# A new opening, score products in groups of two and split last stores in a two-layer decoder trunk

## The chip, the cores and the metric

The kernel runs on one core of a Trainium2 chip. The metric is the device time of one execution in microseconds. The core has a matrix engine (TensorE, PE in the profile), whose products go to eight banks of accumulators (PSUM), three engines for element work (VectorE or DVE, ScalarE or ACT, GpSimd or POOL), and a further one, SyncE or SP, which here only issues transfers. ScalarE can issue transfers too, in between its own work. The engines run side by side, each in its own order, and wait for one another by semaphores.

## What is computed

A trunk of two layers on 512 tokens of 1024 features, in float32. Each layer is

```python
h = rmsnorm(x, norm_mix[l]);   x = x + hybrid_mixer(h, w_in[l], ...)
h = rmsnorm(x, norm_xattn[l]); x = x + cross_attention(h, rmsnorm(mem, norm_mem[l]), ...)
h = rmsnorm(x, norm_mlp[l]);   x = x + sq_relu_mlp(h, mlp_w1[l], mlp_w2[l])
```

and a last `rmsnorm` closes it. The mixer multiplies `h` with the wide matrix `w_in` and cuts the product into columns for four branches: an mLSTM (`m_q`, `m_k`, `m_v`, `m_o` and two narrow gates), GLA (`g_q`, `g_k`, `g_v`, `g_r` and the narrow `g_a`), an S5 state-space model (`s_u`) and HGRN2 (`r_q`, `r_f`, `r_i`, `r_g`). HGRN2 and GLA are the same linear attention with a decay for every key feature, in chunks of 64 positions:

```python
decay = exp(where(causal, g[t] - g[s], -inf))           # per key feature
att   = einsum('bhtk,bhsk,bhtsk->bhts', q, k, decay)
o     = einsum('bhtk,bhkv->bhtv', q * exp(g), S) + einsum('bhts,bhsv->bhtv', att, v)
```

The branches' outputs are projected, weighted by sigmoid gates, summed and projected once more.

## The kernel before

**Dense products.** Each float32 operand is split into a high and a low half, and a product is three (high by high, low by high, high by low). Weights come in units of 128x512 through a ring of nine slots, `WR`. SyncE loads them (L596 and on), ScalarE copies the high half (`feed`, L1429), GpSimd subtracts it to get the low half in two pieces (L694, L695). TensorE takes the units block by block (`parts`, `gemm`, `token_values`); a unit in the usual form gives 12 products, each of 128x512. The order of blocks is written out by hand in TensorE's program: `r_i` with `g_v`, `r_f`, `r_q`, `g_qk`, `g_r`, `r_g`, `gate3_0`, `m_q`, `m_k`, `m_v`, `m_o`, and so on. All products go through the helper at L701, so a line tells little there; the operands' names tell the place. VectorE's helpers for element work stand at L1965 to L1974.

**Opening.** Four tiles of 128 tokens of `x` come in two halves each: tiles 0 and 2 on SyncE's queue (L538), 1 and 3 on ScalarE's. On SyncE's queue there follow the `norm_mix` row (L540, behind a wait for a VectorE memset), unit 0 in two halves (L624: columns of `r_i` and of `g_v`), the second halves of tiles 0 and 2 (L641), then further units. TensorE turns the `norm_mix` row (L964) and the tiles (L944, `x_columns`: tile by tile for the first four groups of features, later group by group). ScalarE scales each turned group into `Uhi` (L1595), VectorE makes its low half and a copy of it (L1974, L2157). `token_values` multiplies groups 0 and 1 for two token tiles and asks for both halves of weights and data before its first product. ScalarE also sums the squares of `x` (L1602); VectorE turns the scales into a diagonal (L1971), which TensorE multiplies, and `h` comes out of that in eight groups: ScalarE's high half (`norm_hi`, L1493, each group behind the `feed` of one more unit, 8 to 15) and VectorE's low half. `values_out` (L1501) empties the banks of `r_i` and `g_v`; `r_f` needs the first of them and `h`.

**Parameters.** After unit 8, SyncE issues `mem`, the level masks and all small parameter rows of layer 0 (`param_rows`, L545 to L580), at their head two loads of `s5_log_step` (L547) that spread 8 numbers over 64 partitions, four bytes a piece; those of layer 1 come three with each unit from 13 to 21. TensorE turns the rows of layer 0 (`params`, L949) ahead of `r_f`, and needs all 23 loads. After unit 12 come two narrow columns of `w_in` (L634), after unit 14 three kinds of loads for the S5 and GLA parameters (L665).

**Level scores.** HGRN2 (`hg`) and GLA (`gl`) form `att` in seven levels: `level_diff` (VectorE), `level_exp` (ScalarE, L1540), `level_mul` (VectorE, L1965 and L1974), `scores` (TensorE, 32 small products a level from 1 up) and `pick` (VectorE, L2081, L2091), which copies the level's part into `att` and frees its banks. The scores stand between parts of dense blocks, one level at a place. After the last level ScalarE copies the turned keys of GLA (`kt_copy`), behind the last tanh of the mLSTM's convolution.

**End.** ScalarE scales the last `out` tiles' first half (L1957) and stores it (L1958), VectorE and SyncE do the second half (L2801, L685), one transfer for each tile and half.

## Time and profile before

| what | value |
|---|---|
| median of 3 runs | 1950.54 us (1949.77, 1950.54, 2742.4) |
| the profiled execution's own time | 1949.91 us |
| its span, first to last instruction | 1948.1 us |
| TensorE's granted clock, mean | 0.999 |
| busy share PE, DVE, ACT, POOL | 99%, 64%, 49%, 58% |

The span is what the trace holds; the time also has what lies around it, 1.8 us. Times in the rows are counted from the span's start. A row of the timeline is a run of like instructions with its start, its length, and in brackets the idle time before it and what ended it. Dense products overlap: a row of 0.39 us starts 0.23 us after the one before. The third run, 2742.4 us, stands apart from the other two.

### The profile page before, as it was taken

What the parts mean: (1) busy time and instruction counts of PE and PEld (TensorE: products, weight loads), DVE (VectorE), ACT (ScalarE), POOL (GpSimd) and SP (SyncE); (2) the same over time, 40 slices, a digit from 0 to 9 for tenths busy, and PEclk for the clock granted to TensorE, in tenths of its full rate; (3) what the DMA queues carried; (4) which work ended last, traced back from release to release, by engine and by line L of the source; (5) the groups of instructions that cost most, each with busy time, mean ns of one, the idle gap of its engine ahead of it and who ended that gap; (6) DMA issues with size and microseconds to landing.
All of it is one profiled execution on the core that took longest, in us unless ns stands there. A gap on an engine that the chain in (4) does not pass through costs nothing.

```text
span 1948.1 us, 33275 instructions
## 1 busy us (share of the span) xinstructions
PE 1931.3 (99%) x12707; PEld 1641.5 (84%) x12707; DVE 1249.7 (64%) x1909; ACT 961.8 (49%) x1665; POOL 1127.9 (58%) x1356
## 2 busy tenths in 40 slices
PE   7999999999999999999999999999999999999998
PEld 6788788888888889999887887888898888999997
DVE  5888778856145766767358786787641556667661
ACT  6754645345445644444456647353554655344334
POOL 4565564956834555766565555467576355566653
PEclk9999999999999999999999999999999999999999
DMA  6423233333422333333342233333343233333332
GB/s 187 119 73 85 82 83 88 87 109 107 148 82 81 99 99 102 99 103 98 98 102 79 72 87 82 81 83 87 120 130 124 66 98 95 111 104 98 103 98 81
DMA packets 196091, 191.41 MB, mean 98 GB/s; under 512 B 23834, under 2 KB 186204, under 8 KB 195548
## 3 DMA queue, kind: packets, MB, share of 16 engines
q1 hardware_dynamic: 194780, 187.19, 32.7%
q8 instruction: 101, 1.65, 0.3%
q10 hardware_dynamic: 1152, 2.10, 0.3%
q14 instruction: 58, 0.48, 0.1%
HBM read 185.04 MB, written 3.15 MB: 97 GB/s over the span
## 4 chain that ended last, share of the span: by engine, by line
PE 95%; ACT 2%; DVE 2%; DMA 1%; issue 0%; SPq 0%; POOL 0%; DVEq 0%; ACTq 0%
PE gemm L701 73%; PE mix L701 20%; DMA w_raw<-in_w_in_dram 1%; DVE work L1974 0%; DVE work L1965 0%; PE mix L1283 0%; DMA work<-in_norm_mix_dram 0%; DVE sums_raw L1965 0%; PE mix L944 0%; PE mix L1178 0%; ACT w_hi L1429 0%; ACT work L1819 0%; DMA w_raw<-in_mlp_w_dram 0%; PE mix L877 0%; ACT work_split L1579 0%
## 5 line engine op out<-in xcount | busy, mean ns | idle before, releaser
L694 POOL TENSOR_TENSOR w_lo<-w_raw,w_hi 128x256 fp32r<-128x256 f32 x676 | 584.8, 865 | 793.0 <-ACT w_hi L1429 793.0
L695 POOL TENSOR_TENSOR w_lo<-w_raw,w_hi 128x256 fp32r<-128x256 f32 x676 | 595.8, 881 | 0.0
L701 PE MATMUL gemm<-h_hi,w_hi 128*128 128x512 f32 x1248 | 493.7, 396 | 0.5 <-DVE h_lo L1974 0.5
L701 PE MATMUL gemm<-h_lo,w_hi 128*128 128x512 f32 x1248 | 486.2, 390 | 0.0
L701 PE MATMUL gemm<-h_hi,w_lo 128*128 128x512 f32 x1248 | 486.1, 390 | 0.0
L701 PE MATMUL gemm<-work_split,w_hi 128*128 128x512 f32 (+1 forms) x1552 | 446.9, 373 | 0.3
L1429 ACT ACTIVATE w_hi<-w_raw 128x512 fp32r<-128x512 f32 x676 | 380.0, 622 | 62.8 <-DMA w_raw<-in_w_in_dram 24.6
L701 PEld LDWEIGHTS gemm<-work_split,w_hi 128*128 128x128 f32 x1552 | 281.6, 189 | 51.0 <-DVE work_split L1974 1.1
L701 PE MATMUL gemm<-work_split,w_lo 128*128 128x512 f32 (+1 forms) x776 | 288.5, 372 | 0.0
L701 PEld LDWEIGHTS gemm<-h_hi,w_hi 128*128 128x128 f32 x1248 | 234.3, 188 | 56.7 <-issue 6.6
L701 PEld LDWEIGHTS gemm<-h_hi,w_lo 128*128 128x128 f32 x1248 | 234.3, 188 | 49.5
L701 PEld LDWEIGHTS gemm<-h_lo,w_hi 128*128 128x128 f32 x1248 | 234.5, 188 | 47.3 <-issue 1.0
L701 PEld LDWEIGHTS gemm<-work_split,w_lo 128*128 128x128 f32 x776 | 146.2, 188 | 25.4
L1427 ACT ACTIVATE gate_rows<-sums_raw 128x768 fp32r<-128x768 f32 x48 | 40.7, 848 | 196.5 <-DVE sums_raw L1965 196.5
L1965 DVE TENSOR_TENSOR work<-work 128x512 f32<-128x512 f32 (+5 forms) x142 | 124.7, 878 | 14.3 <-ACT work L1638 6.5
L701 PE MATMUL mix<-work_split,w_hi 128*128 128x256 f32 (+1 forms) x544 | 121.1, 286 | 0.2 <-DVE sums_lo L1974 0.2
L1965 DVE TENSOR_TENSOR x_t<-x_t,gemm 128x512 f32<-128x512 f32 x88 | 60.5, 687 | 92.0 <-PE gemm L701 87.0
L1534 ACT ACTIVATE gate_t<-gemm 128x512 f32<-128x512 f32 x52 | 31.1, 599 | 140.5 <-PE gemm L701 140.1
L701 PE MATMUL mix<-work_split,gate_rows 128*128 128x256 f32 x456 | 97.8, 283 | 0.0
L701 PEld LDWEIGHTS mix<-work_split,w_hi 128*128 128x128 f32 x544 | 91.8, 191 | 3.6 <-issue 1.4
L701 PEld LDWEIGHTS mix<-work 64*64 64x64 f32 (+4 forms) x3136 | 76.9, 128 | 17.7 <-issue 14.4
L701 PE MATMUL mix<-work 64*64 64x64 f32 (+8 forms) x3136 | 84.2, 231 | 0.9 <-DVE work L1974 0.6
(372 smaller groups left out, 2792.9 us busy)
## 6 DMA issues: line engine op xcount, KB each, us to landing
w_raw<-in_mlp_w_dram SPq DMA_DIRECT2D x256, 256.0 KB, 2.7
w_raw<-in_w_in_dram SPq DMA_DIRECT2D x208, 256.0 KB, 2.7
w_raw<-in_xattn_w_kv_dram SPq DMA_DIRECT2D x64, 256.0 KB, 3.0
w_raw<-in_w_branch_dram SPq DMA_DIRECT2D x32, 256.0 KB, 2.7
w_raw<-in_w_out_dram SPq DMA_DIRECT2D x32, 256.0 KB, 2.7
w_raw<-in_xattn_w_q_dram SPq DMA_DIRECT2D x32, 256.0 KB, 2.8
w_raw<-in_xattn_w_o_dram SPq DMA_DIRECT2D x32, 256.0 KB, 2.7
w_raw<-in_w_in_dram SPq DMA_DIRECT2D x32, 128.0 KB, 3.5
```

Source lines behind the costliest of these rows:

```text
L694: pool.tensor_tensor(lo[:, 0:half], raw[:, 0:half], hi[:, 0:half].bitcast(F32), ALU.subtract)
L695: pool.tensor_tensor(lo[:, half:], raw[:, half:], hi[:, half:].bitcast(F32), ALU.subtract).then_inc(split_ready, 1)
L701: return pe.matmul(o, w, a, start=start, stop=stop, skip_group_check=True)
L1427: act.activation(SWhi[d // 2 % 2], SWraw[d // 2 % 2], ACT.Copy)
L1429: act.activation(hi, raw, ACT.Copy).then_inc(split_hi, 1)
L1534: do(act.activation(t[:, b, :], G[s][b][:, :], ACT.Tanh, scale=0.5), th_ready)
L1965: do(dve.tensor_tensor(o, a, b, op), s)
```

## The change

- *First copies.* The `norm_mix` row and the second half of unit 0 are issued by ScalarE, ahead of the second halves of tiles 1 and 3; SyncE no longer waits for the memset. The second halves of tiles 0 and 2 come behind unit 1. TensorE starts with 2.5 float32 products of zeros (`keep_busy`, on an operand that VectorE clears), turns tiles 0, 1, 3 and then 2, and ends with one more product of zeros. In layer 0 `opening` takes the products of groups 0 and 1 by kind (all high by high, then low by high, then high by low), each kind behind its own wait.
- *Transfers.* The four `s5_log_step` loads and the two narrow columns of layer 0 move to ScalarE, between the feeds up to unit 7 and those of units 8 and 9. The parameter rows are spread: five behind each of units 8 to 11, those of layer 1 two behind each of 15 to 24. `mem` comes behind unit 11, the masks behind unit 25 (VectorE waits for them before its first `pick`), the S5 and GLA loads behind unit 26. In layer 0 `norm_hi` feeds a unit behind each copy, not ahead of it, and four groups come before `values_out("r_i")`, not two.
- *Groups of two.* `scores` of levels 1 and 2, 3 and 4, 5 and 6 stand together, in both mixers, and VectorE's work is put in that order. `kt_copy(gl)` stands ahead of the last tanh.
- *End.* The last tile's scaling and stores are cut in two pieces of 256 columns on both paths.

```diff
+        def pieces(t):
+
+            return (slice(0, 512),) if t < TT - 1 else (FIRST, SECOND)
...
-            sp.wait_ge(p_vec, 1)
-            sp.dma_start(Rf(24, 1)[0:KC, 0:P], norm_mix[0].rearrange("(a b) -> a b", b=P)).then_inc(p_x[0], 16)
...
-                for a in range(2):
-
-                    src = s5_log_step[l].rearrange("(t a) -> a t", a=2)[a:a + 1, :]
-                    sp.dma_start(SM[64 * a:64 * a + 64, 16 + 8 * l:24 + 8 * l],
-                                 src.to_broadcast([64, 8]), allow_slow_non_contiguous=True).then_inc(landed, 16)
-                    yield
...
-                        for n in range(2):
+                        for n in range(2 if u else 1):
...
-                    if u == 12 or (L < DEPTH - 1 and (name, part) == ("up1_0", 0)):
-                        nl = L if u == 12 else L + 1
+                    if L < DEPTH - 1 and (name, part) == ("up1_0", 0):
+                        nl = L + 1
...
-                    if u == 0:
+                    if u == 1:
...
                     if u == 8:
+                        sp.wait_ge(p_pe, 1)
+                        rows0, rows1 = param_rows(0, p_rows), param_rows(1, p_x[1])
+                    if 8 <= u < 12:
+                        for _ in range(5):
+                            next(rows0, None)
+                    if u == 11:
                         sp.dma_start(R(20, 4).rearrange("p (t a) b -> p t (a b)", t=2),
                                      mem[0].rearrange("(t p) d -> p t d", p=P)).then_inc(p_rows, 16)
-                        sp.dma_start(LM[:, :, :], level_masks.rearrange("p (l c) -> p l c", c=CH)).then_inc(p_rows, 16)
-                        sp.wait_ge(p_pe, 1)
-                        for _ in param_rows(0, p_rows):
-                            pass
-                        rows1 = param_rows(1, p_x[1])
                         sp.wait_ge(p_pe, 7)
-                    if 13 <= u < 22:
-                        for _ in range(3):
+                    if 15 <= u < 25:
+                        for _ in range(2):
                             next(rows1, None)
+                    if u == 25:
+                        sp.dma_start(LM[:, :, :], level_masks.rearrange("p (l c) -> p l c", c=CH)).then_inc(p_dma, 16)
                     if u == UNIT["gate3_0"]:
                         sp.wait_ge(p_act, 3)
                         sp.dma_start(mem_scratch, YR[:, 0:4, :].rearrange("p a b -> p (a b)")).then_inc(p_out, 16)
-                    if unit == (14 if L == 0 else 10):
+                    if unit == (26 if L == 0 else 10):
...
-                sp.wait_ge(p_vec, PRO_VEC + TT + t + 1)
-                sp.dma_start(out[0, t * P:(t + 1) * P, 512:], R(2 * t + 1)[:, 0, :]).then_inc(p_out, 16)
-            sp.wait_ge(p_out, 16 + 2 * 16 * TT)
+                for n, at_ in enumerate(pieces(t)):
+                    sp.wait_ge(p_vec, PRO_VEC + TT + t + n + 1)
+                    sp.dma_start(out[0, t * P:(t + 1) * P, 512 + at_.start:512 + at_.stop], R(2 * t + 1)[:, 0, at_]).then_inc(p_out, 16)
+            sp.wait_ge(p_out, 16 + 2 * 16 * (TT + 1))
...
+                def opening(kc, tiles):
+
+                    u, banks = u0 + kc, [(G[(s0, s1)[t // 2]][t % 2][:, :], slice(t * P, t * P + P)) for t in tiles]
+                    w_hi, w_lo = WHi[:, u % RING, :], WLo[:, u % RING, :]
+                    pe.wait_ge(u_hi, kc + 1)
+                    pe.wait_ge(split_hi, u + 1)
+                    for o, tok in banks:
+                        mm(o, Uhi[:, kc, tok], w_hi, start=kc == 0, stop=False)
+                    pe.wait_ge(u_ready, kc + 1)
+                    for o, tok in banks:
+                        mm(o, Ulo[:, kc, tok], w_hi, start=False, stop=False)
+                    pe.wait_ge(split_ready, u + 1)
+                    for o, tok in banks:
+                        mm(o, Uhi[:, kc, tok], w_lo, start=False, stop=False)
...
-                products(0, (0, 1))
-                products(1, (0, 1))
+                for kc in range(2):
+                    if now[0]:
+                        products(kc, (0, 1))
+                    else:
+                        opening(kc, (0, 1))
...
-            pe.wait_ge(p_x[0], 48)
-            pe.transpose(G[0][0][:, 0:P], Rf(24, 1)[:, 0:P], ident).then_inc(p_pe, 1)
-            for t in range(TT):
-                if t:
-                    pe.wait_ge(p_x[t], 16)
-                if t < TT - 1:
-                    x_columns(t, range(4), XB)
-                else:
-                    for k in range(4):
-                        x_columns(t, (k,), XB).then_inc(p_pe, 1)
+            def keep_busy(n):
+                for _ in range(n):
+                    mm(G[1][1][:, :], MG[:, 7, 0:P], MG[:, 7, :])
+
+            pe.wait_ge(v_chain, 1)
+            keep_busy(2)
+            mm(G[1][1][:, 0:256], MG[:, 7, 0:P], MG[:, 7, 0:256])
+            for t in (0, 1, 3):
+                pe.wait_ge(p_x[t], (32, 16, 16, 32)[t])
+                if t == 3:
+                    pe.transpose(G[0][0][:, 0:P], Rf(24, 1)[:, 0:P], ident).then_inc(p_pe, 1)
+                x_columns(t, range(4), XB)
+            pe.wait_ge(p_x[2], 16)
+            for k in range(4):
+                x_columns(2, (k,), XB).then_inc(p_pe, 1)
+            keep_busy(1)
...
+                block = parts("r_g", *H)
+                some(block, 2)
                 pe.wait_ge(*of_layer(gl.gate_in, 2))
                 scores(hg, 1)
-                block = parts("r_g", *H)
-                some(block, 2)
                 scores(hg, 2)
                 rest(block)
-                scores(hg, 3)
                 block = gate_parts(3, 0)
                 some(block, 2)
+                scores(hg, 3)
                 scores(hg, 4)
                 rest(block)
-                scores(hg, 5)
                 block = parts("m_q", *H)
                 some(block, 2)
+                scores(hg, 5)
...
-                scores(gl, 1)
                 block = parts("m_o", *H)
                 some(block, 3)
+                scores(gl, 1)
                 scores(gl, 2)
                 rest(block)
                 branch_gemm(3, 0)
-                scores(gl, 3)
                 block = gate_parts(3, 1)
                 some(block, 3)
+                scores(gl, 3)
                 scores(gl, 4)
                 rest(block)
                 branch_gemm(3, 1)
                 block = gate_parts(3, 2)
-                some(block, 1)
+                rest(block)
                 scores(gl, 5)
-                rest(block)
                 scores(gl, 6)
...
             def norm_hi(k0, k1):
                 for k in range(k0, k1):
-                    feed(first_unit("r_i") + 8 + k)
+                    if now[0]:
+                        feed(first_unit("r_i") + 8 + k)
                     act.wait_ge(*of_layer(hx_ready, k + 1))
                     do(act.activation(Hhi[:, k, :], TH[:, k % 2, :] if now[0] else M[1 + k % 2], ACT.Copy), hi_ready)
+                    feed(first_unit("r_i") + 8 + k)
 
...
+            act.wait_ge(p_vec, 1)
+            act.dma_start(Rf(24, 1)[0:KC, 0:P], norm_mix[0].rearrange("(a b) -> a b", b=P)).then_inc(p_x[3], 16)
+            act.dma_start(WR[:, 0, BW:], w_in[0][0:P, COL["g_v"]:COL["g_v"] + BW]).then_inc(raw_in[0], 16)
...
+                if L == 0:
+                    feed(first_unit("r_i") + 8)
+                    for l, landed in ((0, p_rows), (1, p_x[1])):
+                        for a in range(2):
+                            src = s5_log_step[l].rearrange("(t a) -> a t", a=2)[a:a + 1, :]
+                            act.dma_start(SM[64 * a:64 * a + 64, 16 + 8 * l:24 + 8 * l],
+                                          src.to_broadcast([64, 8]), allow_slow_non_contiguous=True).then_inc(landed, 16)
+                    for what, wide, to in (("m_i", 8, 0), ("g_a", RANK, 8)):
+                        src = w_in[0][:, COL[what]:COL[what] + wide].rearrange("(k p) c -> p k c", p=P)
+                        act.dma_start(NW[:, :, to:to + wide], src, allow_slow_non_contiguous=True).then_inc(nw_in, 16)
+                    feed(first_unit("r_i") + 10)
+                first = 6 if L else 4
...
+                        kt_copy(gl)
                     act.wait_ge(*of_layer(ms["cv_ready"], j + 1))
                     do(act.activation(MTHG[j], MQK[j], ACT.Tanh, scale=0.5), ms["mth_ready"])
-                kt_copy(gl)
...
+                for at_ in pieces(t):
+                    do(act.activation(R(2 * t)[:, 0, at_], R(2 * t)[:, 0, at_], ACT.Copy, scale=SM[:, 32 + t:33 + t]))
+                    act.dma_start(out[0, t * P:(t + 1) * P, at_], R(2 * t)[:, 0, at_]).then_inc(p_out, 16)
...
+            do(dve.memset(MG[:, 7, :], 0.0))
...
+                if L == 0:
+                    dve.wait_ge(p_dma, 32)
...
-                pick(hg, 1)
                 level_diff(hg, 4)
                 gate_out("g_r", gl.GR)
                 level_mul(hg, 3)
+                level_mul(hg, 4)
+                pick(hg, 1)
                 pick(hg, 2)
                 level_diff(hg, 5)
-                level_mul(hg, 4)
-                pick(hg, 3)
                 level_diff(hg, 6)
                 gate_out("r_g", hg.GR)
                 level_mul(hg, 5)
+                level_mul(hg, 6)
+                pick(hg, 3)
                 pick(hg, 4)
-                level_mul(hg, 6)
                 last_decay(hg)
+                decayed(hg)
                 pick(hg, 5)
-                decayed(hg)
...
                 level_mul(gl, 1)
+                level_mul(gl, 2)
                 pick(gl, 0)
                 level_diff(gl, 3)
-                pick(gl, 1)
+                level_diff(gl, 4)
                 do(dve.tensor_copy(pr(17), Ur[:, S5_T, :]))
```

## Rows read from the trace of the kernel before

**Rows 1.** page, part 1: busy time, share of the span and instructions of each engine

```profile
PE 1931.3 (99%) x12707; PEld 1641.5 (84%) x12707; DVE 1249.7 (64%) x1909; ACT 961.8 (49%) x1665; POOL 1127.9 (58%) x1356
```

**Rows 2.** waits of PE, whole run: engine, line, what for; us in total, times, longest

```profile
PE gemm L964 <- DMA work<-in_norm_mix_dram: 7.5, 1, 7.5
...
PE mix L701 <- DVE work L1974: 0.6, 2, 0.3
...
PE mix L701 <- issue: 0.4, 2, 0.2
...
PE mix L701 <- DVE params_all L2211: 0.3, 1, 0.3
```

**Rows 3.** timeline of PE from 7 us: start, length, instructions, idle before and its end

```profile
7.73 3.28 PE L944 MATMUL mix<-consts_sb,work 128*128 128x128 f32 x16
...
12.31 0.50 PE L701 MATMUL gemm<-w_hi,work_split 128*128 128x512 f32 x1 [1.31 <-DVE merged_split L1974]
...
15.91 1.04 PE L944 MATMUL mix<-consts_sb,work 128*128 128x128 f32 x8
```

**Rows 4.** timeline of PE, 37 to 48 us

```profile
37.75 0.47 PE L701 MATMUL gemm<-h_hi,w_hi 128*128 128x512 f32 x1
...
47.42 0.50 PE L701 MATMUL gemm<-h_hi,w_hi 128*128 128x512 f32 x1 [0.54 <-DVE h_lo L1974]
```

**Rows 5.** transfers issued near 1.64 and from 2.6 us: KB each, median us to landing

```profile
work<-in_x_dram SPq DMA_DIRECT2D x1, 256.0 KB, 5.6
...
w_raw<-in_w_in_dram SPq DMA_DIRECT2D x2, 128.0 KB, 5.7
```

**Rows 6.** windows: stretch, length, busy PE PEld DVE ACT POOL, clock, DMA share, GB/s

```profile
7.46:10.50 3.04, 3.04 (x14) 3.04 (x15) 0.17 (x1) 0.63 (x1) 0.81 (x2) 1.00 1.08 386
```

**Rows 7.** timeline of ACT in the opening

```profile
10.72 1.41 ACT L1595 ACTIVATE work_split<-mix,params_all 128x512 fp32r<-128x512 f32 x2 [1.10 <-PE mix L944]
...
12.16 0.63 ACT L1429 ACTIVATE w_hi<-w_raw 128x512 fp32r<-128x512 f32 x1
...
30.62 0.60 ACT L1493 ACTIVATE h_hi<-mix 128x512 fp32r<-128x512 f32 x1 [4.83 <-DVE mix L1974]
```

**Rows 8.** timeline of POOL in the opening

```profile
9.69 0.73 POOL L694 TENSOR_TENSOR w_lo<-w_raw,w_hi 128x256 fp32r<-128x256 f32 x1 [9.25 <-ACT w_hi L1429]
```

**Rows 9.** timeline of DVE in the opening

```profile
24.02 2.74 DVE L1971 TENSOR_SCALAR work<-consts_sb,small 128x128 f32<-128x128 f32 x4
...
31.41 0.69 DVE L1974 SCALAR_TENSOR_TENSOR h_lo<-mix,h_hi 128x512 fp32r<-128x512 f32 x1
```

**Rows 10.** timeline of SP, 32 to 41 us

```profile
32.85 1.29 SPq L547 DMA_DIRECT2D small<-in_s_log_step_dram  x2
...
35.57 4.88 SPq L555 DMA_DIRECT2D work<-in_norm_mem_dram  x1
```

**Rows 11.** transfers in the window from 35 to 40 us: packets and bytes

```profile
DMA packets 542, 0.00 MB, mean 0 GB/s; under 512 B 542, under 2 KB 542, under 8 KB 542
```

**Rows 12.** timeline of PE around a group of HGRN2's scores

```profile
96.65 0.39 PE L701 MATMUL gemm<-h_hi,w_lo 128*128 128x512 f32 x1
...
96.97 1.15 PE L701 MATMUL mix<-work 128*64 128x64 f32 x32
...
98.05 0.50 PE L701 MATMUL gemm<-h_hi,w_hi 128*128 128x512 f32 x1
```

**Rows 13.** timeline of PE, GLA's scores of level 2

```profile
170.65 0.69 PE L701 MATMUL mix<-work 64*64 64x64 f32 x32
```

**Rows 14.** timelines of DVE and ACT, 157 to 168 us

```profile
157.43 1.91 DVE L2081 COPY_PREDICATED work<-masks_sb,mix 128x256 f32<-128x256 int32 x4
...
162.46 0.63 ACT L1540 ACTIVATE work<-work 128x512 f32<-128x512 f32 x1
...
165.58 1.72 DVE L1974 SCALAR_TENSOR_TENSOR work<-work,consts_sb 128x256 f32<-128x256 f32 x2
```

**Rows 15.** timeline of ACT at the end

```profile
1944.08 0.72 ACT L1957 ACTIVATE work<-work,small 128x512 f32<-128x512 f32 x1
```

More of the change, by code:

```diff
@@ L947, in params @@
             def params(l):
-                pe.wait_ge(p_x[1] if l else p_rows, 16 * 22 if l else 16 * 23)
+                pe.wait_ge(p_x[1] if l else p_rows, 16 * 22)
                 pe.transpose(M[3 - l][:, 0:P], Rf(24 + l, 1)[:, 0:P], ident).then_inc(p_pe, 1)
@@ L1599, in _ @@
                     t = k - 1
-                    act.wait_ge(p_x[t], 48 if t == 0 else 16)
+                    act.wait_ge(p_x[t], (32, 16, 16, 32)[t])
                     act.wait_ge(p_x2, 16 * TT)
@@ L1611, in _ @@
                 factors(0)
-                first = 6 if L else 2
+                if L == 0:
[10 more added lines that the diff above has]
+                first = 6 if L else 4
                 norm_hi(0, first)
@@ L1618, in _ @@
                 if L == 0:
-                    act.wait_ge(p_rows, 16 * 23)
+                    act.wait_ge(p_rows, 16 * 22)
                     for t in range(2):
@@ L1956, in _ @@
                 fdo(act.activation(SM[:, 32 + t:33 + t], SM[:, 32 + t:33 + t], ACT.Exp, scale=-0.5))
-                do(act.activation(R(2 * t)[:, 0, :], R(2 * t)[:, 0, :], ACT.Copy, scale=SM[:, 32 + t:33 + t]))
-                act.dma_start(out[0, t * P:(t + 1) * P, 0:512], R(2 * t)[:, 0, :]).then_inc(p_out, 16)
+                for at_ in pieces(t):
+                    do(act.activation(R(2 * t)[:, 0, at_], R(2 * t)[:, 0, at_], ACT.Copy, scale=SM[:, 32 + t:33 + t]))
+                    act.dma_start(out[0, t * P:(t + 1) * P, at_], R(2 * t)[:, 0, at_]).then_inc(p_out, 16)
         @block.vector
@@ L2300, in _ @@
                 tt(Ui[:, :, :], Ui[:, :, :], PS[:, 8:8 + S5_T + 1, :], ALU.mult)
-                level_mul(gl, 2)
-                level_diff(gl, 4)
-                pick(gl, 2)
                 tt(pr(5), re_, re_, ALU.mult)
@@ L2318, in _ @@
                 level_mul(gl, 4)
+                pick(gl, 1)
+                pick(gl, 2)
                 level_diff(gl, 5)
                 level_diff(gl, 6)
-                pick(gl, 3)
                 merge(3, 0)
@@ L2324, in _ @@
                 conv(1)
-                pick(gl, 4)
                 level_mul(gl, 5)
                 level_mul(gl, 6)
+                pick(gl, 3)
+                pick(gl, 4)
                 def silu_of(j):
@@ L2334, in _ @@
                 conv(2)
+                merge(3, 1)
                 pick(gl, 5)
                 decayed(gl)
-                merge(3, 1)
+                pick(gl, 6)
                 conv(3)
@@ L2340, in _ @@
                 silu_of(1)
-                pick(gl, 6)
                 decayed_queries(gl)
@@ L2800, in _ @@
                 dve.wait_ge(p_act, PRO_ACT + t + 1)
-                dve.scalar_tensor_tensor(out=R(2 * t + 1)[:, 0, :], in0=M[t], scalar=SM[:, 32 + t:33 + t], in1=GAINS[1],
-                                         op0=ALU.mult, op1=ALU.mult).then_inc(p_vec, 1)
+                for at_ in pieces(t):
+                    dve.scalar_tensor_tensor(out=R(2 * t + 1)[:, 0, at_], in0=M[t][:, at_], scalar=SM[:, 32 + t:33 + t], in1=GAINS[1][:, at_],
+                                             op0=ALU.mult, op1=ALU.mult).then_inc(p_vec, 1)
 _INS = ['x', 'mem', 'norm_mix', 'w_in', 'mlstm_conv_w', 'mlstm_conv_b', 'mlstm_i_bias', 'mlstm_f_bias', 'mlstm_norm',
```

## The prediction

> **What bounds the kernel now.** I read the page's first part, then who TensorE waited for over the whole run, then the order of time around each edited place. TensorE has work in flight for 1931.3 of 1948.1 us [rows 1], and the waits left to it are the reader's first surprise: 7.5 us for the `norm_mix` row before its first instruction, 0.3 us for `params_all`, 0.6 us in two waits for a VectorE product, 0.4 us in two waits before the turned keys' products [rows 2], and 0.5 us for the last low half of `h` [rows 4]. The rest is pace: products of 128x512 start about 0.23 us apart. So this kernel can only gain by starting its dense stretch sooner, by losing fewer steps where one kind of product follows another, and by a shorter end. All of that together is about 1% of the time; 2% of 1950 us is 39 us, more than the edited stretches hold.
>
> The opening has three places to see. The first 16 turns of `x` take 3.28 us, the next 8 only 1.04 us, so the first ones ran at half pace; the first dense product starts at 12.31 us, after a wait of 1.31 us for the low half, and its group of 12 ends at 15.91 us [rows 3]. The block `r_f` starts at 37.75 us and stands still once, 0.54 us before 47.42 us [rows 4]; between those TensorE keeps its pace.
>
> **The change, part by part.**
>
> *First copies.* The second half tile of `x` on SyncE's queue is issued at 1.64 us and lands 5.6 us later, at 7.2 us; the two halves of weight unit 0, issued behind the `norm_mix` row, land at the median 5.7 us after issues at 2.5 and 2.9 us, at 8.0 and 8.9 us [rows 5]. Afterwards the `norm_mix` row and the second half are on ScalarE's queue, ahead of the rest of `x`, and SyncE waits for nothing. How soon unit 0 is then complete no row shows: 7.2 us is the lower bound (with the tile ahead of it), 8.9 us the upper. I take 7.8 us, 256 KB at the 386 GB/s that the stretch from 7.46 us moves [rows 6] behind the tile. ScalarE copies unit 0 (0.63 us) and the first turned tile (0.7 us, half of the two in 1.41 us [rows 7]) and is done at 9.2 us instead of 11.4. `opening` starts with the products that need no low halves, but its last pair needs unit 1's low half: ScalarE copies tile 1 and unit 1 until 10.5 us and GpSimd takes two halves of 0.73 us after it [rows 8], so the group of 12 ends near 12.6 us, not 15.91: **3.3 us sooner**. The early zero products cost nothing: by the columns of the first turns (3.28 us for 16 x 128 [rows 3]) their 1280 columns take 2.1 us, or 4.1 if each column costs double, and with VectorE's memset of their operand early in the run both fit ahead of 7.2 us; what they may give is the better pace of the last four turns, 0.4 us, which is in this sum. Should they not lift the pace, the sum loses these 0.4 us. If unit 0 comes at 8.9 us, the gain is 2.2 us.
>
> *The rest of the opening.* TensorE would come to `r_f` at 37.75 - 3.3 = 34.4 us. On the way it needs the diagonal that VectorE builds until 26.76 us [rows 9] out of ScalarE's squares, which move up by some 1.7 us. TensorE gains 3.3, so the diagonal's slack of today shrinks by 1.6 us. TensorE does not wait for it today [rows 2]; I count nothing, and up to 1.6 us if there is no slack.
>
> *Six more issues on ScalarE.* ScalarE now idles 4.83 us before the first `h` copy at 30.62 us [rows 7]. Into that hole go unit 7, four `s5_log_step` loads, two narrow columns of `w_in`, and units 8 and 9. Its copies up to there are one string behind the first turned tile, so it comes to the first issue 1.3 to 2.2 us sooner than it came to the hole at 30.62 - 4.83 = 25.8 us: at 24.5 us, to take the later. Every issue holds the engine, and behind it stand the four `h` copies, then `values_out("r_i")`, which frees the bank that `r_f` writes: TensorE waits for that. The lower bound of the six: six at the pair's 0.64 us, 3.9 us [rows 10], so units 8 and 9 (1.25 us) end at 29.6 us, before the first `h` copy begins today: nothing is lost. But what TensorE also awaits for `params(0)`, the landing of the first two loads, is slow: in five microseconds only 542 packets move, 108 per us, while two such loads have 1024 [rows 11], so they need 9.5 us and land at 24.5 + 1.5 (the estimated way in) + 9.5 = 35.5 us; `r_f` starts then, 2.3 us sooner than now. The upper bound: an issue behind such loads can stick. SyncE's fourth issue after the pair (the sixth of six) took 4.88 us and ended at 40.45 us, 7.6 us after the first of the pair began [rows 10]. ScalarE has four of these loads and two larger lists behind them. If it is held until the third or the fourth load is through (1536 or 2048 packets at 108 per us), it is free at 40.2 or 45 us. The row nearest to this case is the 4.88 us one, because there too the sixth issue of a string follows these loads: I take a hold until 24.5 + 7.6 = 32.1 us. Units 8 and 9 then last to 33.4, the first `h` copy to 34.0, VectorE's pairs of passes (0.69 us each [rows 9], 1.45 a pair with their gaps) put the fourth copy at 37.5, and the first bank is free at 38.3 us: `r_f` **0.55 us later** than now.
>
> *After `r_f` has started.* The wait of 0.54 us inside it [rows 4] goes, about 0.7 us with the drain and refill around it: `h` no longer waits for unit 14, since ScalarE copies the units behind `h` and not ahead of it, and the slow loads have left SyncE's queue. The 0.3 us for `params_all` goes too, since ScalarE has done the squares of `mem` before `r_f` ends. The loads moved behind units 25 and 26 (masks, `s5_b`, `s5_c`, `WA2`) are issued as the units ahead of them get their slots, well before the block `g_r` whose masks and scores need them: nothing, unless that queue is late by a whole block. That opening in all: 0.55 - 0.7 - 0.3 = **-0.45 us**.
>
> *Groups of two.* A group of 32 score products today costs more than its own work: the product ahead takes 0.32 instead of 0.23 us, the first behind 0.50 instead of 0.39, and the group 1.08 us from 96.97 to 98.05, of which some 0.15 is the wait for its last product to end [rows 12]. GLA's groups are shorter, 0.69 us [rows 13], with the same two borders. A second group appended to a first spares one such border: 0.20 us for the two steps, 0.32 with a last product's end. Each layer has three places fewer for each of the two mixers: 12 x 0.32 = **3.8 us** (bounds 2.4 and 3.8). The odd level now comes later, so that its operands are never late: the two waits of 0.3 us for a product (0.35 each with the drain) go. `pick(gl, 6)` and ScalarE's copy of the turned keys stand ahead of a conv and a tanh, so the two waits of 0.2 us go. Together **1.1 us**. What could replace them: both levels 1 and 2 of GLA must be ready where level 2 stands today, 170.65 us, less the 0.8 us by which level 1 no longer stands ahead [rows 13]. ScalarE's exponent for level 2 ends at 163.1 us; VectorE's product for it (2.6 us: three passes, of which two take 1.72) and the pick of 1.91 us end at 167.6 us [rows 14]: some 2 us to spare.
>
> *Last stores.* The scaling of the last tile takes 0.72 us from 1944.08 us [rows 15]. In halves of some 0.4 us the first store goes 0.3 us sooner and the last about 0.5 us later with a quarter of the 512 KB behind it instead of all, which take 1.36 us at the 386 GB/s of [rows 6]. Between a loss of 0.5 and a gain of 0.7 I take **0.4 us** gained, because the second piece is issued while the first is moving.
>
> The sum: -0.45 - 3.8 - 1.1 - 0.4 = -5.75 us against the profiled execution's 1949.91 us, which lies between two of the runs shown (1949.77 and the median 1950.54; the third, 2742.4, is no measure of the program): **1944.2 us**.
>
> **The rivals.** *ScalarE is hardly held* (A). For it: its own queue has been empty since the last of `x`, and the pair's two issues took 1.29 us together [rows 10]. Then `r_f` starts at 35.5 us: -2.3 - 1.0 - 5.3 = -8.6, 1941.3 us.
> *ScalarE is held long* (C), which ends on the other side: free at 40.2 or 45 us, `r_f` at 46.4 or 51.2, 8.7 or 13.5 us later, less 6.3 for the rest: +2.4 or +7.2, 1952 or 1957 us. It decides from the point where the six issues last 14 us, ScalarE free at 38.2 and `r_f` at 44. For it speaks that there are twice as many slow packets as in the row; against it that SyncE was let go when half of them were through.
> *The order of transfers moves nothing* (D). For it: the DMA engines are already full at 386 GB/s when unit 0 lands [rows 6], so more queues bring no more bytes. Then the first dense group stays at 12.31 us, ScalarE has its issues in today's hole, and what is left is the waits of 0.7 and 0.3 and the 5.3 us: 1943.6 us, if that hole still holds them. Against it: it is not the bytes but the place of the `norm_mix` row and of the second half that changes. The Trainium skill has a rule for it, "DMA: Bandwidth & Descriptors", section "Issuing engines are not separate DMA queues": loads from several engines share the same DMA engines, and spreading them saves only issue time. By that rule the time would be this rival's. The row of the pair speaks half against it: what was queued behind it on the same queue waited, which the rule alone does not tell.
> *A pair waits* (E): the product for levels 1 and 2 of GLA comes 2 us past its slack in both layers: +4, 1948 us.
>
> **How the numbers follow.** The forecast 0.35, A 0.32, C 0.16 (half of it under 1951 us), D 0.07, E 0.05, something not seen 0.05. The forecast's own range is 1942.5 to 1947. For 8 in 10 the range goes down to 1939.5 (A with unit 0 at its lower bound) and up to 1951 (most of C's shorter holds left in). All cases stay within 2%, what a measurement of this kernel can tell from no change: faster 0.01, same 0.97, slower 0.02, these two for what is not seen.
>
> **What would show it.** Right: `r_f` starting at 38 us with ScalarE's issue rows stretched to some 7 us in all; 128x64 groups of 64; no wait of TensorE for a product near 177 us. A is right if those rows end by 28.5 us. The forecast is wrong if TensorE's first dense group ends after 14 us, if ScalarE's rows end after 38 us, or if a new wait stands at a pair.

## The result

The changed kernel takes 1956.62 us (median of 6 runs, 1954.94 to 1957.65), the kernel before 1950.01 us (median of the 6 runs now at hand; one of them, 2742.4 us, stands apart). The ratio is 1.0034 with a 95% interval of 1.002 to 1.0048: the kernel became slower by 0.34%, some 6.6 us. Forecast were 1944.2 us, and the range ended at 1951. Within 2% of the kernel before it stays, as said. The profiled execution took 1957.61 us with a span of 1955.8 us, 7.7 us more than before.

Where TensorE now waits, over the whole run (columns: engine, line, what for; us in total, times, longest), where [rows 2] has before:

```profile
PE gemm L702 <- ACTq L1529: 12.4, 1, 12.4
PE mix L968 <- DMA small<-in_s_log_step_dram: 3.0, 1, 3.0
PE gemm L702 <- DVE merged L2185: 1.8, 1, 1.8
PE mix L702 <- DVE sums_lo L2015: 0.3, 1, 0.3
```

All the small waits of [rows 2] are gone, and one new place costs 15.4 us. L968 turns the parameters, L1529 is ScalarE's signal at the end of `values_out("r_i")`. Both stand ahead of `r_f`. The timeline of PE there, against the first of [rows 4]:

```profile
37.71 0.45 PE L968 MATMUL mix<-consts_sb,work 128*128 128x128 f32 x1 [3.00 <-DMA small<-in_s_log_step_dram]
50.57 0.79 PE L702 MATMUL gemm<-h_hi,w_hi 128*128 128x512 f32 x1 [12.41 <-ACTq L1529]
51.16 0.63 PE L702 MATMUL gemm<-h_lo,w_hi 128*128 128x512 f32 x1
...
54.57 0.44 PE L702 MATMUL gemm<-h_hi,w_hi 128*128 128x512 f32 x1
54.85 0.40 PE L702 MATMUL gemm<-h_lo,w_hi 128*128 128x512 f32 x1
```

`r_f` starts at 50.57 us, not 37.75 [rows 4], and its first nine products start 0.43 us apart, not 0.23. The windows of the same stretch (stretch, length, busy PE PEld DVE ACT POOL, clock, DMA share, GB/s) show why the latter:

```profile
37.70:50.57 12.87, 0.45 (x2) 0.17 (x2) 4.82 (x7) 4.63 (x8) 3.37 (x5) 0.50 0.37 85
50.57:54.57 4.00, 4.00 (x9) 3.13 (x10) 3.33 (x6) 3.68 (x7) 2.65 (x5) 0.50 0.00 0
54.57:60.00 5.43, 5.43 (x25) 4.47 (x24) 3.47 (x6) 5.18 (x10) 3.81 (x6) 0.99 0.31 71
```

While TensorE stood still its granted clock went to 0.50, and it stayed there for the first 4 us of work: 1.85 us more than before over those products.

What held ScalarE, in its timeline (against [rows 7]):

```profile
23.68 2.86 ACTq L1646 DMA_DIRECT2D small<-in_s_log_step_dram  x4
26.58 17.17 ACTq L1650 DMA_DIRECT2D work<-in_w_in_dram  x2
43.80 1.15 ACT L1453 ACTIVATE w_hi<-w_raw 128x512 fp32r<-128x512 f32 x2 [19.50 <-issue]
44.85 1.21 ACT L1518 ACTIVATE h_hi<-mix 128x512 fp32r<-128x512 f32 x2
```

The four step loads were issued in 2.86 us, the two narrow columns in 17.17 us. Only then came units 8 and 9 and the first `h` copy, at 44.85 us instead of 30.62. What moved meanwhile, in the window from 28 to 34 us (packets of all queues; then queue, packets, MB, share of 16 engines; then a transfer with its size and us to landing):

```profile
DMA packets 680, 0.03 MB, mean 6 GB/s; under 512 B 658, under 2 KB 677, under 8 KB 680
...
q10 hardware_dynamic: 656, 0.00, 4.8%
...
w_raw<-in_w_in_dram SPq DMA_DIRECT2D x2, 256.0 KB, 16.7
```

ScalarE's queue (q10) moved 656 packets of four bytes in 6 us, 109 per us, the pace of [rows 11]; they fill 4.8% of the 16 DMA engines' time. (A packet in this view is a piece of a transfer in the text.) The two weight units that SyncE issued in that stretch (14 and 15) landed 16.7 us after their issue, at the median.

Since the dense products come in the same order but for the first twelve, their starts can be subtracted one from another. After minus before, in us:

| at | after - before | step |
|---|---|---|
| end of the first dense group (12.76 against 15.91) | -3.15 | the opening |
| first product of `r_f` | +12.81 | ScalarE held, TensorE stopped: +16.1 from -3.28 |
| tenth product of `r_f` | +14.66 | half clock: +1.85 |
| behind the place of the 0.54 us stop | +14.05 | stop gone: -0.6 |
| ahead of `g_r`'s second part | +13.56 | `params_all` and small steps: -0.5 |
| behind layer 0's groups | +10.72 | -2.84 |
| ahead of layer 1's groups | +10.57 | -0.15 |
| behind layer 1's groups | +7.72 | -2.85 |
| end of the span | +7.7 | some 0.2 lost on the way, the stores -0.2 |

So all parts but one gain about what was worked out, 10 us together, and one loses 18.

### The profile page after: what moved, and what is told of

Read it like the earlier page. It is cut to its first block, busy times and chain, and to the rows that moved or that the text cites. A ratio compares the mean times of both kernels' runs of the same rounds, so it can differ in the third digit from the quotient of the medians.

```text
span 1955.8 us, 33296 instructions
## 1 busy us (share of the span) xinstructions
PE 1932.7 (99%) x12715; PEld 1643.4 (84%) x12715; DVE 1248.0 (64%) x1911; ACT 959.9 (49%) x1666; POOL 1118.5 (57%) x1356
## 3 DMA queue, kind: packets, MB, share of 16 engines
HBM read 185.04 MB, written 3.15 MB: 96 GB/s over the span
## 4 chain that ended last, share of the span: by engine, by line
PE 96%; ACTq 1%; DVE 1%; ACT 1%; DMA 0%; issue 0%; DVEq 0%
PE gemm L702 74%; PE mix L702 20%; ACTq L1650 1%; PE mix L1307 0%; DVE sums_raw L2006 0%; ACT w_hi L1453 0%; PE mix L1202 0%; DVE work L2015 0%; DMA w_raw<-in_mlp_w_dram 0%; ACT work L1859 0%; PE mix L896 0%; ACT work_split L1605 0%; ACTq L1646 0%; DVE h_raw L2006 0%; PE mix L1396 0%
## 5 line engine op out<-in xcount | busy, mean ns | idle before, releaser
L695 POOL TENSOR_TENSOR w_lo<-w_raw,w_hi 128x256 fp32r<-128x256 f32 x676 | 580.6, 859 | 810.5 <-ACT w_hi L1453 810.5
L696 POOL TENSOR_TENSOR w_lo<-w_raw,w_hi 128x256 fp32r<-128x256 f32 x676 | 588.0, 870 | 0.0
L1453 ACT ACTIVATE w_hi<-w_raw 128x512 fp32r<-128x512 f32 x676 | 379.3, 621 | 75.6 <-issue 19.5
L702 PEld LDWEIGHTS gemm<-work_split,w_lo 128*128 128x128 f32 x776 | 146.2, 188 | 25.5
```

Source lines behind the costliest of these rows:

```text
L695: pool.tensor_tensor(lo[:, 0:half], raw[:, 0:half], hi[:, 0:half].bitcast(F32), ALU.subtract)
L696: pool.tensor_tensor(lo[:, half:], raw[:, half:], hi[:, half:].bitcast(F32), ALU.subtract).then_inc(split_ready, 1)
L702: return pe.matmul(o, w, a, start=start, stop=stop, skip_group_check=True)
L1453: act.activation(hi, raw, ACT.Copy).then_inc(split_hi, 1)
```

## The experiments

All ratios are to runs of the kernel before on the same chip (medians 1949.99, 1950.31 and 1950.21 us for the three groups of four).

**Who issues, and what stands ahead.** Three kernels put issues of the changed kernel back to SyncE; the fourth keeps all six on ScalarE and changes the shape of the step loads.

*e1: all six back on SyncE, at the places they had before.*

```diff
 def param_rows(l, landed):
+    for a in range(2):
+        sp.dma_start(SM[64*a:64*a+64, ...], <every second number of s5_log_step[l], spread over 64>)
...
-    if L < DEPTH - 1 and (name, part) == ("up1_0", 0):
+    if u == 12 or (L < DEPTH - 1 and (name, part) == ("up1_0", 0)):   # narrow columns
...
-    act.dma_start(...)   # six issues of ScalarE
```

> The changed kernel with the four step loads (4-byte pieces) and the two narrow columns issued by SyncE again, at the places they had before; all else as changed. In the changed trace ScalarE's two narrow issues last 17.2 us and r_f starts at 50.57 us, 16.1 us behind the 34.5 at which TensorE was ready, and 1.85 us more go at half clock after the stop. Theory H (what costs is that ScalarE is held in its issues): both go, 1956.6 - 16.1 - 1.85 = 1938.7 us, or 1942 if r_f still waits for the first step loads until 37.7. Rival S (the 4-byte pieces make every transfer late, whichever engine issues them): the weight units 9 and 10, now on the same queue, are late as before, r_f starts after 45 us, 1951 us or more.

Measured: 1941.81 us, ratio 0.9958 (0.9941 to 0.9974). TensorE's waits of the run, but for its start:

```profile
PE mix L707 <- DVE params_all L2250: 1.0, 1, 1.0
PE mix L707 <- DVE work L2003: 0.4, 1, 0.4
```

`r_f` starts at 35.06 us without a stop, and the time is far under the 1951 of S. It lies between H's two values, near the upper, but not for that value's reason: no wait for the step loads came. Of the 3.1 us over the lower value the two waits shown are 1.4; the rest is not traced.

*e2: the step loads on SyncE, the narrow columns on ScalarE.*

> The changed kernel with only the four step loads back on SyncE; ScalarE still issues the two narrow columns between units 7 and 8. Theory H, with the cause that the narrow lists wait behind 4-byte pieces on their own queue: their two issues take some 1.1 to 4 us, r_f starts between 34.5 and 38 us, 1939 to 1942 us. Rival N (a list of 1024 short pieces holds its issuer by itself): the two issues last about 17 us as now, r_f near 50, 1955 us.

Measured: 1941.42 us, ratio 0.9956 (0.9941 to 0.9971). ScalarE's timeline:

```profile
23.81 1.58 ACTq L1650 DMA_DIRECT2D work<-in_w_in_dram  x2
```

The same two issues that lasted 17.17 us last 1.58 us. Rival N falls: a narrow list alone holds nobody.

*e3: the narrow columns on SyncE, the step loads on ScalarE.*

> The changed kernel with only the two narrow columns back on SyncE, behind unit 12; ScalarE issues the four step loads. Theory H: ScalarE's issues take 2.9 us as now and it is free at 26.6 us; r_f waits for the first two step loads alone, near 37.7 us, 1942 us. Rival S: unit 9, which ScalarE copies ahead of h, lands at 41.9 us as now because the 4-byte pieces delay it on the other queue; r_f then starts at about 41.9 + 6.8 = 48.7 us, 1954 us. Rival N gives what H gives.

Measured: 1947.56 us, ratio 0.9987 (0.9978 to 0.9996), between the two theories. ScalarE's issues, and TensorE's timeline at `r_f`:

```profile
23.83 4.01 ACTq L1646 DMA_DIRECT2D small<-in_s_log_step_dram  x4
```

```profile
38.39 0.45 PE L968 MATMUL mix<-consts_sb,work 128*128 128x128 f32 x1 [3.51 <-DMA small<-in_s_log_step_dram]
38.59 0.77 PE L702 MATMUL gemm<-h_hi,w_hi 128*128 128x512 f32 x1
```

ScalarE is free at 27.84 us, 1.2 us later than H says: its fourth step load took 1.89 us, against 0.70 in the changed kernel. The course is H's: `r_f` waits for the first two step loads alone, 3.5 us, and then runs at half clock for some products, 2.4 us by the products' starts. H left out that second price and 0.8 us of a wait for `params_all`; from e4 below, which has none of the three, 1939.95 + 3.5 + 2.4 + 0.8 = 1946.7 us, 0.9 us under the measured median (two more small waits, 0.2 and 0.3 us, are in this trace and not in e4's). S was worked out with a wrong reading, in e1 as here: the units that land late are not 9 and 10 but 13 and 14, which ScalarE copies behind `h` and `r_q` needs. What S says of them is so: unit 13, issued from 25.82 us on, landed at 48.26 us. It was only not needed sooner.

*e4: the step loads in whole rows, all six on ScalarE as changed.* VectorE picks every second number while it copies.

```diff
-src = s5_log_step[l].rearrange("(t a) -> a t", a=2)[a:a + 1, :]
-act.dma_start(SM[64 * a:64 * a + 64, 16 + 8 * l:24 + 8 * l], src.to_broadcast([64, 8]), ...)
+act.dma_start(SM[64 * a:64 * a + 64, 16 * l:16 * l + 16],
+              s5_log_step[l].rearrange("(a b) -> a b", a=1).to_broadcast([64, 16]))
...
-dve.tensor_copy(PTA[:, l, step:step + 8], SM[:, 16 + 8 * l:24 + 8 * l])
+for a in range(2):
+    dve.tensor_copy(PTA[64 * a:64 * a + 64, l, step:step + 8], <columns a, a + 2, ... of SM[64 * a:64 * a + 64, 16 * l:16 * l + 16]>)
```

> The changed kernel with each step load made of whole rows: 64 pieces of 64 bytes in place of 512 of 4, issued at the same place by ScalarE, and VectorE picks every second number when it copies them. If the 4-byte pieces are the cause (H with them, and S): ScalarE's six issues take about 4 us, nothing is late, r_f starts at 34.5 to 36 us, 1939 to 1941 us. Rival N: the narrow lists hold ScalarE as now, 1955 us.

Measured: 1939.95 us, ratio 0.9949 (0.9934 to 0.9963): the fastest, 10 us under the kernel before and 16.7 under the changed one. ScalarE's issues, TensorE's two waits of the whole run, and `r_f`:

```profile
23.98 2.58 ACTq L1645 DMA_DIRECT2D small<-in_s_log_step_dram  x4
26.59 1.70 ACTq L1649 DMA_DIRECT2D work<-in_w_in_dram  x2
```

```profile
PE gemm L702 <- DVE merged L2184: 1.8, 1, 1.8
PE gemm L702 <- ACT work_split L1624: 0.5, 1, 0.5
```

```profile
34.86 0.27 PE L968 MATMUL mix<-consts_sb,work 128*128 128x128 f32 x1
35.24 0.50 PE L702 MATMUL gemm<-h_hi,w_hi 128*128 128x512 f32 x1
```

Same engine, same place, same order, as many issues: only the pieces of the step loads differ, 64 a load in place of 512, and VectorE's short copies of them. The stop and the half clock are gone. The cause is the 4-byte pieces. It is not their number alone, since in e2 two lists of 1024 pieces of 32 and 64 bytes held nobody; whether it is their size or that they take every second number of the source no run separates.

**How long a queue of them holds its issuer.** The two narrow issues of the changed kernel, one by one:

```profile
26.58 7.80 ACTq L1650 DMA_DIRECT2D work<-in_w_in_dram  x1
34.42 9.33 ACTq L1650 DMA_DIRECT2D work<-in_w_in_dram  x1
```

Counted in the trace, they ended when some 2120 and 2170 pieces were open, that is, issued and not yet moved (the packets that report a landing have four bytes too and are counted with them). Two kernels try the count.

*e9: the two narrow columns ahead of the four step loads.*

> The changed kernel with the two narrow columns issued ahead of the four step loads, all on ScalarE at the same place. Counted in the changed trace, 954 and 1924 of the 4-byte pieces had moved when the first and the second narrow issue ended, at 34.38 and 43.75 us: 3072 - 954 = 2118 and 4096 - 1924 = 2172 pieces were then issued and not yet moved. Theory R (an issuer is let go when no more than about 2150 pieces of its queue are open): the narrow pieces, which moved at some 500 a microsecond, make room, ScalarE is free by 32 us, and r_f waits for the landing of the first two step loads, 39 to 41 us, plus some 2 us of half clock: 1944 to 1947 us. Rival L (an issue waits for all that stands ahead of it in the queue to land): the last step load waits for three others, 14 us, ScalarE free at 40 us or later, r_f at 47, 1953 us.

Measured: 1947.33 us, ratio 0.9986 (0.9977 to 0.9995). ScalarE's issues and TensorE's wait:

```profile
24.09 1.03 ACTq L1645 DMA_DIRECT2D work<-in_w_in_dram  x2
25.16 8.12 ACTq L1649 DMA_DIRECT2D small<-in_s_log_step_dram  x4
```

```profile
PE mix L968 <- DMA small<-in_s_log_step_dram: 6.9, 1, 6.9
```

ScalarE is free at 33.3 us, a little later than R said and far ahead of L. The step loads land later instead, at 42 us, and the time is just above R's upper end. The execution in this trace was the slowest of the ten, 1950.12 us, so its holds and its wait can be longer than those of the median run.

*e10: two step loads and one narrow column on ScalarE, the other three on SyncE.*

> The changed kernel with only the two step loads of layer 0 and the first narrow column on ScalarE (1024 + 1024 pieces); those of layer 1 and the second narrow column are on SyncE where they were before. Theory R: never more than 2048 pieces are open on ScalarE's queue, its three issues take 2 to 3 us, and r_f waits for the step loads' landing at 35 to 37.7 us: 1940 to 1944 us. Rival L: the narrow issue waits until most of the 1024 slow pieces have moved, 8 us, ScalarE free at 34 us, r_f at 41, 1947 us.

Measured: 1943.36 us, ratio 0.9967 (0.9955 to 0.9978).

```profile
23.84 1.37 ACTq L1651 DMA_DIRECT2D small<-in_s_log_step_dram  x2
25.24 0.64 ACTq L1655 DMA_DIRECT2D work<-in_w_in_dram  x1
```

With at most 2048 pieces open, an issue right behind 1024 slow pieces took 0.64 us. L falls. What is left is 2.7 us of TensorE's wait for the landing, and half clock in the window behind it:

```profile
37.77:40.40 2.63, 2.63 (x7) 2.12 (x7) 1.80 (x3) 2.40 (x4) 2.29 (x4) 0.50 0.23 60
40.50:43.00 2.50, 2.50 (x13) 2.05 (x12) 1.96 (x3) 2.47 (x4) 1.82 (x3) 1.00 0.05 0
```

R doesn't tell all. The first step load of e9 took 4.61 us and was let go with some 600 pieces open, the fourth took 2.12 us though the queue never held more than 2048 then, and so did e3's fourth, 1.89 us. SyncE was held for 5.04 us by a row of 8 pieces in the changed kernel (at 34.78 us), with three weight units ahead of it. In e9's trace one of the sixteen shares of a transfer was late: when the first step load was let go, 56 of the first narrow list's pieces and 64 of the second's were left, about a sixteenth of each, and of the sixteen landing signals of a weight unit in the same stretch fifteen came by 27.89 us and one at 30.15. An issue that waits for the fullest of sixteen shares, and not for the sum, would fit; no run tests it. What sets the room of a queue, and that of its neighbour, stays open.

**The other parts, one at a time.**

*e5: the kernel before with the groups of two and the order around them alone.*

> The kernel before with the groups of two alone (TensorE's places of the scores, VectorE's order, the copy of the turned keys ahead of the last tanh); opening, transfers and end as before. The prediction's sum for this part is 3.8 + 1.1 = 4.9 us: 1945.1 us. The traces of before and after, compared product by product, give it more: 1.1 + 1.7 us in layer 0 and 2.85 us in layer 1, 5.7 us in all: 1944.3 us. If the groups gain only because the opening has moved the loads, under 2 us.

Measured: 1944.41 us, ratio 0.997 (0.9958 to 0.9981), 5.9 us. By the products' starts in its trace the groups give 5.7 us again (2.8 and 2.9 in the two layers); its opening also gained 0.7 us there and a wait of 2.4 us for `h` cost more than before. A pair in the changed kernel, against [rows 12]:

```profile
108.90 0.39 PE L702 MATMUL gemm<-h_hi,w_lo 128*128 128x512 f32 x1
109.22 2.09 PE L702 MATMUL mix<-work 128*64 128x64 f32 x64
111.23 0.50 PE L702 MATMUL gemm<-h_hi,w_hi 128*128 128x512 f32 x1
```

64 products in 2.01 us from start to start; twice 1.08 and one more border of 0.2 would be 2.36.

*e6: the kernel before with the step loads in rows alone.*

> The kernel before with the step loads made of 64 whole rows of 64 bytes in place of 512 pieces of 4 bytes, on SyncE at the old places; all else as before. If the 4-byte pieces already held the kernel before: unit 14 no longer lands 10.6 us after its issue, the stop of 0.54 us inside r_f goes (0.6 to 0.7 us with drain and refill), and the wait for params_all of 0.3 us may go: 1949.0 to 1949.4 us. If the stop comes from the order of the feeds alone: 1950.0 us.

Measured: 1949.44 us, ratio 0.9996 (0.9987 to 1.0005): not settled by the times. In its trace TensorE waits no more for `h` nor for `params_all` (the two gain 1.2 us by the products' starts), but its opening happened to run 1.2 us later than in the trace of before, 0.3 us of it the row's landing.

*e7: e4 without the products of zeros.*

```diff
-keep_busy(2)
-mm(G[1][1][:, 0:256], MG[:, 7, 0:P], MG[:, 7, 0:256])
...
-keep_busy(1)
```

> The changed kernel with the step loads in rows (1939.95 us), without the products of zeros ahead of and behind the first turns. If TensorE's pace in the opening comes from the work ahead of it: the first 16 turns take about 3.3 us again in place of 1.75 us, the first dense group starts and runs slower, 0.5 to 1.5 us lost: 1940.5 to 1941.5 us. If the zeros do nothing: 1940.0 us.

Measured: 1940.01 us, ratio 0.9949 (0.9936 to 0.9963), the time of e4. PE's opening without the zeros, and then with them (e4):

```profile
5.47 1.94 PE L963 MATMUL mix<-consts_sb,work 128*128 128x128 f32 x8 [5.47 <-DMA work<-in_x_dram]
7.21 0.42 PE L990 MATMUL gemm<-consts_sb,work 128*128 128x128 f32 x1
7.42 1.91 PE L963 MATMUL mix<-consts_sb,work 128*128 128x128 f32 x8
9.47 0.80 PE L702 MATMUL gemm<-w_hi,work_split 128*128 128x512 f32 x1
```

```profile
6.11 1.04 PE L963 MATMUL mix<-consts_sb,work 128*128 128x128 f32 x8
6.98 0.27 PE L992 MATMUL gemm<-consts_sb,work 128*128 128x128 f32 x1
7.09 1.04 PE L963 MATMUL mix<-consts_sb,work 128*128 128x128 f32 x8
7.96 1.02 PE L702 MATMUL gemm<-merged 128*128 128x512 f32 x2
9.45 0.73 PE L702 MATMUL gemm<-w_hi,work_split 128*128 128x512 f32 x2 [0.47 <-ACT work_split L1624]
```

The zeros do give the turns their full pace, eight in 1.04 us and not 1.94; the granted clock is 1.00 in both stretches, so the rows do not show why. But the first dense product starts at 9.45 or 9.47 us: it waits for ScalarE, whose first copy ends at 9.4 us in both, not for the turns.

*e8, e12: e4 with the last tile's scaling and stores whole.*

> The changed kernel with the step loads in rows (1939.95 us), the last tile's scaling and stores whole again. By the prediction's term 0.4 us slower, 1940.35 us; by the difference of the traces' ends (span behind the last dense product 0.2 us shorter in the changed kernel), 1940.15 us; if the pieces cost their second issue, 1939.5 us.

> The same with the last tile's scaling and stores whole, on the same chip as the run above: 0.2 us slower by the traces' ends, 0.4 us by the prediction's term.

> The changed kernel with the step loads in rows once more, for its time and as the pair of the next run: 1939.6 to 1940.3 us.

Measured: 1940.4 (e8) and 1940.38 us (e12), and 1940.2 us for e4 once more beside e12 (e11): 0.2 us of difference, less than the runs of one kernel differ (1939.65 to 1940.43), so the times don't settle it. ScalarE's end in the changed kernel, against [rows 15]:

```profile
1951.99 0.51 ACT L1998 ACTIVATE work<-work,small 128x256 f32<-128x256 f32 x1
1952.53 0.35 ACTq L1999 DMA_DIRECT2D out_dram<-work  x1
1952.93 0.51 ACT L1998 ACTIVATE work<-work,small 128x256 f32<-128x256 f32 x1 [0.43 <-ACT work L1998]
1953.47 0.34 ACTq L1999 DMA_DIRECT2D out_dram<-work  x1
```

## Why the prediction was wrong

**The step that failed** is the hold of ScalarE: "The row nearest to this case is the 4.88 us one, because there too the sixth issue of a string follows these loads: I take a hold until 24.5 + 7.6 = 32.1 us." ScalarE came to its first issue at 23.68 us (24.5 worked out) and was free at 43.75: a hold of 20.1 us where 7.6 was taken. The upper bound of the same paragraph, free when the fourth load is through, was 45 us. The row of 4.88 us [rows 10] was like this case in its place in a string; it was unlike it in what counts, the number of slow pieces ahead (1024, not 2048) and the size of what came behind (short rows, not two lists of 1024). The pace of 108 pieces a microsecond, which [rows 11] already showed, was right to 1%. With it, a room of some 2150 open pieces gives the length of this hold, from which that number was counted; e10 agrees, while e9 and e3 have holds that it does not give.

**The rival that came true** is C: free at 45, `r_f` at 51.2, 1957 us; measured were 43.75, 50.57 and 1956.62. It had a chance of 0.16, and the range stopped at 1951, short of both times that C itself gave. That its time agrees so closely is in part luck, since errors of its sum cancel: the half clock behind the stop (1.85 us) was not foreseen, while `r_f` came 0.6 us sooner than it says and the groups gave 0.8 us more than was counted. Its reason, that there are twice as many slow pieces as in the row, was the right one; the argument against it, that SyncE was let go when half of them were through, did not carry over: there the last issue was a short row, here lists of 1024 pieces. The bound that was worked out for the full load belonged inside the range. A slip that decides nothing: by the working's own 6.2 us from ScalarE's release to `r_f`, 44 us is reached when the six issues last 13.3 us, not 14.

**The landing of the first step loads**: 35.5 us worked out, 37.7 us measured (the wait at L968). The way in had no row behind its 1.5 us; the first piece moved at 26.29 us, 2.6 us behind the first issue. And the loads did not land one after the other: when the last of the first two had landed, 1294 packets of four bytes had moved on the queue, and the two loads are 1024. It would have cost 3 us by itself, as e3 and e10 show (3.5 and 2.7 us, and half clock on top).

**The opening**: right. ScalarE's first two copies were done at 9.23 us (9.2 worked out), the first dense group ended at 12.76 us (12.6), TensorE would have come to `r_f` at 34.5 (34.4). The share of the zeros in it was wrong: the 0.4 us for the pace of the last turns is nothing (e7), the first dense product waits for ScalarE's copies. The diagonal was ready at 25.28 us and wanted at 25.5: hidden, by 0.2 us.

**After the start of `r_f`**: the stop of 0.54 us went (0.6 by the starts, 0.7 worked out), the wait for `params_all` too. In e1 and e2, where the slow loads are back on SyncE, a wait for `params_all` of 1.0 us stands again: it goes with the slow pieces (e3 has it too, 0.8 us, e4 and e6 have none) and not with ScalarE's order alone. The stop needed only one of the two reasons given: it is gone in e1, where the slow loads are on SyncE, and in e6, where ScalarE's order is the old one.

**Groups of two**: the mechanism was right, the size was low: 3.8 + 1.1 = 4.9 us worked out, 5.7 in the traces, 5.9 by the times of e5. HGRN2's three places gave 1.12 us in layer 0 (13.56 to 12.44 by the starts), 0.37 each where 0.32 was taken; the working's own two numbers, 0.20 and 0.15, give 0.35. No wait took the place of the old ones (rival E falls).

**Last stores**: 0.4 us worked out, 0.2 by the ends of the traces, and not more than the times can tell. ScalarE's second scaling waits for its first issue, and starts 0.94 us after the first; its last store is issued 1.48 us after the scaling began, where the whole tile's scaling took 0.72 [rows 15].

**Rival D**, that the order of transfers moves nothing, falls with the 3.15 us of the first group. The rule of the Trainium skill named there ("DMA: Bandwidth & Descriptors", section "Issuing engines are not separate DMA queues") says that transfers run on the same DMA engines whoever issues them. The traces bear out that the queues are not apart: while the slow pieces moved on ScalarE's queue, SyncE's weight units were late (16.7 us to landing, and landing at 48.26 us for unit 13 in e3); why, with the DMA engines mostly idle, they don't show. The Trainium skill also says there that issuing from several engines saves only the time of issuing, which is usually small. Here that time was a cost and not small: ScalarE, which has other work, stood idle for 19.5 us in its issues.

## What to carry to other kernels

Before an issue is moved onto an engine that computes, look at the number and the size of the transfer's pieces and not at its bytes alone: behind 8 KB in 4-byte pieces two further issues held ScalarE for 17 us. Better than to move such a load is to load whole rows and let an element engine pick the numbers; that took 16.7 us off the changed kernel. When the rows near an unknown differ from it in load, the bound at the full load belongs in the range.

## What the runs showed of the hardware

- Four-byte pieces moved at 109 per us on a queue and filled 4.8% of the 16 DMA engines' time (the changed kernel, 28 to 34 us). With the step loads in rows (e4), the same queue moved 2211 packets, most of them of 32 and 64 bytes, in the 5 us from 25 to 30 us.
- While such pieces moved on one queue, the other was slow: weight units of 256 KB needed 16.7 us to land there, 2.7 us in the median of the run.
- An issue came back in 0.64 us with 2048 pieces open on its queue (e10), and only after 7.8 and 9.3 us where 3072 and 4096 had been issued in all, with some 2120 and 2170 open at the end. This is no fixed threshold: e9 and e3 have longer issues with fewer pieces open.
- In TensorE's stops of 3 us (e10) and 16 us (the changed kernel) the granted clock went to 0.50, 1.2 GHz, and the first 2.6 and 4.0 us of work behind them still ran at that level. The price of a stop was more than its length, by 1.2 and 1.85 us, and by 2.4 us behind the 3.5 us of e3.
